# A mixture-of-experts layer on one core: one stationary for the two parts of each expert's 48-row block, with GpSimd's and VectorE's order changed around it

## Chip, core and metric

The kernel runs on one core of a Trainium2 chip. The time is device microseconds of one execution; the table gives the median of three runs. The five engines are TensorE (PE), VectorE (DVE), ScalarE (ACT), GpSimd (POOL) and SyncE (SP). Times inside a profile count from the span's start.

## What is computed

A transformer layer over 1024 rows of 1024 numbers, in float32: a mixer, a cross attention and a grouped mixture of experts, each followed by a layer norm. The change lies in the last part alone:

```python
y = jnp.zeros_like(t)
for e in range(N_EXPERTS):                      # 16 experts, D_EXPERT = 256
    h = jax.nn.silu(t @ w_gate[e]) * (t @ w_up[e])
    y = y + combine[:, e:e + 1] * (h @ w_down[e])
x = layer_norm(DEEPNORM_ALPHA * x + y, ln_moe_g[l], ln_moe_b[l])
```

A router picks a group of four experts for each row and two experts in it, so combine has two entries that are not zero in a row.

## The kernel before

Up to 692 us of the span the kernel works through projection, attention and cross attention and sorts the rows into slots: each of the 16 experts has CAP = 176 slots, whose rows lie in a DRAM buffer (slot_rows, `xs_dram`). The function `experts` then takes the experts one after the other, one step each. The first four and the last two are written out, the ten between run in a loop of two. The 176 rows of an expert stand as a block c = 0 of 128 rows and a block c = 1 of 48 rows (`B1`). A step goes as follows.

TensorE computes gate and up for half m = 0 and m = 1 of the 256 hidden columns into h_ps (L2004), turns the next expert's rows with `turn` (L1985, L1987) into rowsT_ps, and computes the down product into y_ps (L2016 to L2018). Float32 precision of down is had from three products of fp32r parts: h_hi with e_dn_hi, h_hi with e_dn_lo, h_lo with e_dn_hi. So each block c, each half j of the 1024 output columns and each half f of the hidden columns takes three matmuls over 512 columns, 24 in a step. The four sums (c, j) share three banks of y_ps; (1, 1) takes the bank of (0, 0) once VectorE has read it.

ScalarE makes silu (L2055), h_hi (L2058), copies the turned rows to xgT (L2039, L2040), makes e_dn_hi for the next expert (L2044) and, from the fifth expert on, the sum of squares of each row for the layer norm (L2071).

VectorE multiplies silu by up (L2128), makes h_lo (L2130), writes the finished rows of the expert before with `put_out` (L2097, both blocks behind the second h_lo), works out which slots hold a row's second expert (`know_high`, `place`), makes the row sums z = y x weight + earlier sum with their accumulators (L2147, four passes over 512 columns), the means (L2102), `centre` (L2108), and splits the next e_dn into e_dn_lo (L2082, four passes). A row's low expert stores z to a DRAM buffer (slot_sums, `z_dram`), and its high expert, at least four steps later, takes that z as the earlier sum. The first four experts have no high rows and so no layer norm.

GpSimd reads weight and ids of the next expert's slots (`read_fields`, L1922, L1924), gathers the earlier sums with two indirect DMAs over the rows in SBUF (`gather_low`, L1929), makes rstd from the squares (L1950, L1953), and scatters the finished rows to out with two indirect DMAs as `put_out` has made them (L1956). Then it waits until they have landed and only then signals `out_free`, on which the next `put_out` waits.

SyncE issues the next e_down_raw load when e_dn_lo is made, the gate and up load two experts ahead when gate and up are done, the two stores of z as they are made, and behind them the two fetches of the rows of the expert after next (L1898, L1880):

```python
for c in range(2):
    hold(z_made, n(4, 2 * c + 6))
    sp.dma_start(k.z_dram[bass.ds(n(CAP, c * P), ROWS[c]), :], z[c][:]).then_inc(z_stored, 16)
if not is_one_of_last(e, 2):
    hold(placed_at, n(1, 1))
    fetch(n(CAP, 2 * CAP), b)
```

All semaphore values are written out by hand: n, h and g_ turn the step's number into the count to wait for. Each engine works its list in order, so a wait holds up all that stands behind it on that engine.

## Time and profile before

| | us |
|---|---|
| median of 3 runs | 977.92 (973.67 to 980.97) |
| profiled execution | 977.82 |
| its span | 976.0 |
| TensorE busy | 941.4, 96% of the span |
| VectorE busy | 591.0, 61% |
| ScalarE busy | 350.9, 36% |
| GpSimd busy | 196.5, 20% |
| mean granted TensorE clock | 0.99 of 2.4 GHz |

The profile is of one execution. Matmuls are pipelined and their ends are modelled, so it is the distance of their starts that tells their cost. The experts take the span from 692 us to the end. In the rows further down a row of a timeline gives start, duration, engine, line, operation, result and inputs; in brackets stands how long the engine was idle before it and what ended the idle time.

### The profile page before, as it was taken

To read this page: it belongs to the slowest core of one execution; us is meant where nothing else is said; L and a number is where in the kernel's file an instruction comes from. 1 tells how busy PE (TensorE), PEld (TensorE's weight loads), DVE (VectorE), ACT (ScalarE), POOL (GpSimd) and SP (SyncE) were. 2 spreads that over 40 slices of the span, in tenths; PEclk is the share of its full clock that TensorE was granted. 3 is DMA by queue.
4 is the path that set the end of the run, shared out by engine and by line. 5 is a ranking of instruction groups with operands and counts; after the bars stand their busy time and mean duration, and the time that the engine had idled before them with its cause. 6 is when DMAs were issued, how large, how long until landed. Compare 5 with 4: busy or idle time off the path is not lost. (4 is left out here: it accounts for less than half of the span.)

```text
span 976.0 us, 15660 instructions
## 1 busy us (share of the span) xinstructions
PE 941.4 (96%) x5655; PEld 798.5 (82%) x5655; DVE 591.0 (61%) x1263; ACT 350.9 (36%) x737; POOL 196.5 (20%) x256
## 2 busy tenths in 40 slices
PE   7999999999999999999999999998999999999993
PEld 6899888778778888888868888878889898989882
DVE  6744341588677775756656455476343567677674
ACT  6123031345575555300043333320322334444441
POOL 0013100122241120122200000005200243342444
PEclk9999999999999999999999999999899999999998
DMA  9122010001699502600223000046688989898962
GB/s 306 64 87 87 1 62 5 1 1 41 255 412 378 177 23 66 259 1 1 87 90 130 1 1 1 16 158 255 232 293 249 318 280 299 289 323 323 308 247 91
DMA packets 67278, 151.60 MB, mean 155 GB/s; under 512 B 8720, under 2 KB 16144, under 8 KB 67216
## 3 DMA queue, kind: packets, MB, share of 16 engines
q1 hardware_dynamic: 59920, 133.82, 39.0%
q0 software_dynamic: 7296, 16.95, 4.6%
q8 instruction: 39, 0.64, 0.3%
q14 instruction: 23, 0.19, 0.1%
HBM read 107.62 MB, written 52.03 MB: 164 GB/s over the span
## 5 line engine op out<-in xcount | busy, mean ns | idle before, releaser
L2004 PEld LDWEIGHTS h_ps<-xgT,e_gate_up 128*128 128x128 f32 x1024 | 155.6, 192 | 4.7 <-issue 2.4
L2004 PE MATMUL h_ps<-xgT,e_gate_up 128*128 128x176 f32 x1024 | 157.1, 315 | 2.4 <-DVEq L2112 2.4
L270 PE MATMUL unit_ps<-whi,xhi 128*128 128x512 f32 (+1 forms) x256 | 98.2, 384 | 6.1 <-DVE wlo L308 6.1
L271 PE MATMUL unit_ps<-wlo,xhi 128*128 128x512 f32 (+1 forms) x256 | 97.9, 382 | 0.0
L272 PE MATMUL unit_ps<-whi,xlo 128*128 128x512 f32 (+1 forms) x256 | 97.7, 382 | 0.0
L270 PEld LDWEIGHTS unit_ps<-whi,xhi 128*128 128x128 f32 x256 | 48.6, 190 | 13.8 <-DVE xlo L352 6.1
L2147 DVE SCALAR_TENSOR_TENSOR z<-y_ps,slot_weight,x_rows 128x512 f32<-128x512 f32 (+1 forms) x64 | 45.6, 746 | 22.5 <-PE y_ps L2018 21.9
L272 PEld LDWEIGHTS unit_ps<-whi,xlo 128*128 128x128 f32 x256 | 48.6, 190 | 7.8
L271 PEld LDWEIGHTS unit_ps<-wlo,xhi 128*128 128x128 f32 x256 | 48.6, 190 | 7.5
L2016 PE MATMUL y_ps<-e_dn_hi,h_hi 128*128 128x512 f32 (+1 forms) x128 | 52.1, 407 | 0.2
L2018 PE MATMUL y_ps<-e_dn_hi,h_lo 128*128 128x512 f32 (+1 forms) x128 | 50.3, 393 | 0.0
L2017 PE MATMUL y_ps<-e_dn_lo,h_hi 128*128 128x512 f32 (+1 forms) x128 | 50.0, 391 | 0.0
L2128 DVE TENSOR_TENSOR h<-silu_g,h_ps 128x176 f32<-128x176 f32 x32 | 10.7, 333 | 56.7 <-ACT silu_g L2055 56.7
L2055 ACT ACTIVATE silu_g<-h_ps 128x176 f32<-128x176 f32 x32 | 10.2, 318 | 93.0 <-PE h_ps L2004 85.8
L2071 ACT ACTIVATE ln_junk<-z,z_neg_mean 128x1024 f32<-128x1024 f32 (+1 forms) x24 | 27.6, 1152 | 39.8 <-DVE z_neg_mean L2102 33.3
L1046 PE MATMUL t_ps<-constants,prob 128*128 128x128 f32 x288 | 41.2, 279 | 0.6 <-DVE prob_T L1194 0.4
L1063 PEld LDWEIGHTS o_ps<-prob_T,mla_v 128*64 128x64 f32 x576 | 30.8, 136 | 12.9 <-DVE prob_T L1194 8.8
L1063 PE MATMUL o_ps<-prob_T,mla_v 128*64 128x128 f32 x576 | 38.5, 278 | 3.0 <-DVE prob_T L1194 2.4
L2082 DVE TENSOR_TENSOR e_dn_lo<-e_down_raw,e_dn_hi 128x512 fp32r<-128x512 f32 x64 | 39.7, 678 | 0.8 <-ACT e_dn_hi L2044 0.8
L1194 DVE COPY prob_T<-t_ps 128x512 f32<-128x512 f32 (+3 forms) x48 | 29.7, 619 | 14.0 <-PE t_ps L1046 13.9
L1116 ACT ACTIVATE prob_T<-t_ps 128x128 f32<-128x128 f32 (+3 forms) x48 | 21.0, 437 | 46.9 <-PE t_ps L1046 46.9
L2044 ACT ACTIVATE e_dn_hi<-e_down_raw 128x512 fp32r<-128x512 f32 x64 | 35.2, 637 | 5.9 <-DVE ln_tmp L2119 4.4
(346 smaller groups left out, 2136.8 us busy)
## 6 DMA issues: line engine op xcount, KB each, us to landing
e_gate_up<-w_gu SPq DMA_DIRECT2D x16, 2048.0 KB, 10.9
e_down_raw<-w_dn SPq DMA_DIRECT2D x16, 1024.0 KB, 5.7
slot_rows<-zeros SPq DMA_DIRECT2D x22, 522.0 KB, 6.3
slot_sums<-zeros SPq DMA_DIRECT2D x22, 512.0 KB, 6.4
x_rows<-slot_rows SPq DMA_DIRECT2D x16, 522.0 KB, 4.6
slot_sums<-z SPq DMA_DIRECT2D x16, 512.0 KB, 4.1
wraw<-w_in SPq DMA_DIRECT2D x24, 256.0 KB, 4.5
xraw<-xT SPq DMA_DIRECT2D x16, 256.0 KB, 5.1
```

What stands on the lines that cost most here:

```text
L270: pe.matmul(o, hi, whi[:, s, 0:w], start=(s == 0), stop=False)
L271: pe.matmul(o, hi, wlo[:, s, 0:w], start=False, stop=False)
L272: last = pe.matmul(o, lo, whi[:, s, 0:w], start=False, stop=(s == KD - 1))
L1046: last = pe.transpose(tps[:, j, m * P:(m + 1) * P], prob[:, u % 2, j, m * P:(m + 1) * P], ident)
L1063: last = pe.matmul(ops[r, i % 2, (h // 2) * P:(h // 2 + 1) * P], k.v[:, m, h * MV:(h + 1) * MV], src, start=(m == 0), stop=(m == i))
L2004: end = pe.matmul(hps[:, m, gu * CAP:(gu + 1) * CAP], gate_up[:, b, s, w], xT[:, s, :], start=(s == 0), stop=(s == KD - 1))
L2016: pe.matmul(out, hi, dn_hi[:, b, w, :], start=(f == 0), stop=False)
L2017: pe.matmul(out, hi, dn_lo[:, b, w, :], start=False, stop=False)
L2018: return pe.matmul(out, lo, dn_hi[:, b, w, :], start=False, stop=(f == 1))
L2044: act.activation(dn_hi[:, b, s, :], dn_raw[:, s, :], ACT.Copy).then_inc(dn_hi_done, 1)
L2082: dve.tensor_tensor(dn_lo[:, b, s, :], dn_raw[:, s, :], dn_hi[:, b, s, :].bitcast(f32), ALU.subtract).then_inc(dn_lo_done, 1)
L2147: dve.scalar_tensor_tensor(z[c][:, f], yps[r, BANK[u], :], wgt[r, b, c:c + 1], rows[b][r, c, f], ALU.mult, ALU.add, accum_out=zsum[r, c, j ...
```

## The change

The layout of `h_hi` gets room behind the 176 columns: the 48-row block's h_hi stands in columns 128 to 175, zeros in 176 to 191, and its low part in 192 to 239. One matmul with columns 128 to 239 as stationary and e_dn_hi as moving gives the high part's product in partitions 0 to 47 and the low part's in partitions 64 to 111 of the same bank; a second adds h_hi with e_dn_lo to partitions 0 to 47. So 12 matmuls of a step become 8. The two sums of the block get banks of their own, the second of them in rowsT_ps. VectorE adds the two parts in two passes over each half: first low part x weight + earlier sum, then high part x weight + that.

`put_out` is split: block 0 behind the first h multiply, block 1 behind the second half's low parts. GpSimd copies the ids for the scatter to a tile of its own and no longer waits for the scatter to land; `put_out` and that copy wait for the scatter of two experts before. TensorE waits for the row sums of the expert before ahead of its transposes, and for the copy of the turned rows ahead of the last four matmuls. The weights lie in DRAM so that two rows of them stand side by side in one partition (`paired`), 4 KB instead of 2 KB in one piece. `fetch` gets an argument for its blocks, which no call gives.

```diff
+def paired(w):
+    return w.rearrange("p (s t) n -> p s (t n)", t=2)
...
-    hhi = at("h_hi", 146, [P, 2, CAP], f32r)
-    hlo = at("h_lo", 147.5, [P, 2, CAP], f32r)
+    LOW = P + 64
+    hhi = at("h_hi", 150, [P, 2, LOW + B1], f32r)
+    hlo = at("h_lo", 147.5, [P, 2, P], f32r)
...
-    UNITS = [(0, 0), (0, 1), (1, 0), (1, 1)]
-    BANK = [0, 1, 2, 0]
+    BANK = [0, 1]
+        small_sums = [yps[:, 2, :], tps[:, 0, :]]
...
-            def fetch(row, b):
-                for c in range(2):
+            def fetch(row, b, blocks=range(2)):
+                for c in blocks:
...
-                    sp.dma_start(dn_raw[:], A["w_dn"][bass.ds(n(1, 1), 1)].rearrange("a s p n -> p (a s) n")).then_inc(dn_loaded, 16)
+                    sp.dma_start(paired(dn_raw[:]), A["w_dn"][bass.ds(n(1, 1), 1)].rearrange("a s p n -> p (a s) n")).then_inc(dn_loaded, 16)
...
                 pool.tensor_tensor(rs[:], sq[:], half[:], ALU.pow).then_inc(rstd_made, 1)
+                if not lowest(e, 2):
+                    hold(out_scattered[b], h(32, -64))
+                pool.tensor_copy(out_ids[:, b, :], ids[:, b, :, 1]).then_inc(out_ids_made, 1)
+                hold(out_ids_made, g_(1, 1))
                 for c in range(2):
                     hold(out_made, g_(2, c + 3))
-                    pool.indirect_dma_start(A["out"], bass.IndirectOffsetOnAxis(ap=ids[0:ROWS[c], b, c, 1:2], axis=0), o[c][:], None,
-                                            bounds_check=S - 1, oob_is_err=False).then_inc(out_scattered, 16)
-                if not is_one_of_last(e, 2):
-                    hold(out_scattered, g_(32, 32))
-                    pool.sem_inc(out_free, 1)
+                    pool.indirect_dma_start(A["out"], bass.IndirectOffsetOnAxis(ap=out_ids[0:ROWS[c], b, c:c + 1], axis=0), o[c][:], None,
+                                            bounds_check=S - 1, oob_is_err=False).then_inc(out_scattered[b], 16)
...
                 else:
+                    pe.wait_ge(z_made, n(4, 4))
                     turn(1 - b, h(32, 32 * (1 + b)))
...
-                def down(u, f):
-                    c, j = UNITS[u]
+                def down(j, f):
                     w = 2 * f + j
-                    hi, lo = (t[:, f, c * P:c * P + ROWS[c]] for t in (hhi, hlo))
-                    out = yps[0:ROWS[c], BANK[u], :]
+                    hi, lo, out = hhi[:, f, 0:P], hlo[:, f, :], yps[:, BANK[j], :]
...
+                def small_down(j, f):
+                    w, sums = 2 * f + j, small_sums[j]
+                    if f:
+                        pe.matmul(sums[0:B1], hhi[:, f, P:CAP], dn_lo[:, b, w, :], start=False, stop=False)
+                    last = pe.matmul(sums[0:64 + B1], hhi[:, f, P:LOW + B1], dn_hi[:, b, w, :], start=(f == 0), stop=(f == 1))
+                    if f == 0:
+                        last = pe.matmul(sums[0:B1], hhi[:, f, P:CAP], dn_lo[:, b, w, :], start=False, stop=False)
+                    return last
...
-                for u, free in ((0, 4), (1, 2), (2, 3)):
-                    pe.wait_ge(z_made, n(4, free))
-                    down(u, 0)
+                pe.wait_ge(z_made, n(4, 4))
+                down(0, 0)
+                down(1, 0)
+                pe.wait_ge(small_lo_done, n(2, 1))
+                small_down(0, 0)
                 pe.wait_ge(hlo_done, n(2, 2))
-                for u in range(3):
-                    down(u, 1).then_inc(ysum, 1)
-                pe.wait_ge(z_made, n(4, 5))
-                down(3, 0)
-                down(3, 1).then_inc(ysum, 1)
+                down(0, 1).then_inc(ysum, 1)
+                down(1, 1).then_inc(ysum, 1)
+                pe.wait_ge(small_lo_done, n(2, 2))
+                small_down(0, 1).then_inc(ysum, 1)
+                if not last:
+                    pe.wait_ge(x_done, n(1, 2))
+                small_down(1, 0)
+                small_down(1, 1).then_inc(ysum, 1)
...
-            def put_out(n, blocks=range(2)):
+            def put_out(n, h, e, b, blocks):
                 dve.wait_ge(rstd_made, n(1, 1))
-                dve.wait_ge(out_free, n(1, 1))
+                if not lowest(e, 2):
+                    dve.wait_ge(out_scattered[b], h(32, -64))
...
                     dve.tensor_tensor(hh[:, m, :], act_g[:, m, :], hps[:, m, CAP:2 * CAP], ALU.mult).then_inc(hmul, 1)
+                    if not lowest(e) and m == 0:
+                        put_out(g_, h, e, b, [0])
                     dve.wait_ge(hhi_done, n(2, m + 1))
-                    dve.tensor_tensor(hlo[:, m, :], hh[:, m, :], hhi[:, m, :].bitcast(f32), ALU.subtract).then_inc(hlo_done, 1)
-                    if last:
-                        put_out(g_, [m])
-                if not lowest(e) and not last:
-                    put_out(g_)
+                    dve.tensor_tensor(hlo[:, m, :], hh[:, m, 0:P], hhi[:, m, 0:P].bitcast(f32), ALU.subtract).then_inc(hlo_done, 1)
+                    dve.tensor_tensor(hhi[:, m, LOW:LOW + B1], hh[:, m, P:CAP], hhi[:, m, P:CAP].bitcast(f32), ALU.subtract)\
+                       .then_inc(small_lo_done, 1)
+                if not lowest(e):
+                    put_out(g_, h, e, b, [1])
...
+                for j in range(2):
+                    row_sums(j, 0, j, yps[:, BANK[j], :], rows[b][:, 0, 512 * j:512 * j + 512], zsum[:, 0, j:j + 1], z_made)
+                if last:
+                    mean(0, n)
+                for j in range(2):
+                    row_sums(2 + j, 1, j, small_sums[j][64:64 + B1], rows[b][0:B1, 1, 512 * j:512 * j + 512], None, half_made)
+                for j in range(2):
+                    dve.wait_ge(half_made, n(2, j + 1))
+                    row_sums(2 + j, 1, j, small_sums[j][0:B1], z[1][:, 512 * j:512 * j + 512], zsum[0:B1, 1, j:j + 1], z_made)
                 if last:
                     mean(1, n)
+                    centre(0, g_)
                     centre(1, g_)
```

`row_sums` is the pass of L2147 with the sum, the earlier sum and the accumulator given.

## Rows read from the trace of the kernel before

**Rows 1.** The page, part 1: busy time of each engine.

```profile
PE 941.4 (96%) x5655; PEld 798.5 (82%) x5655; DVE 591.0 (61%) x1263; ACT 350.9 (36%) x737; POOL 196.5 (20%) x256
```

**Rows 2.** Windows: stretch, length, each engine's busy us, granted clock, DMA share, GB/s.

```profile
828.12:845.18 17.06, 16.98 (x105) 14.65 (x104) 11.87 (x24) 7.50 (x15) 6.36 (x8) 1.00 0.89 292
...
861.96:878.71 16.75, 16.75 (x106) 14.72 (x105) 11.91 (x24) 7.38 (x15) 6.61 (x8) 1.00 0.91 326
...
945.74:976.00 30.26, 15.54 (x89) 12.99 (x87) 17.56 (x30) 6.31 (x12) 14.46 (x14) 0.84 0.28 96
```

**Rows 3.** Timeline of TensorE, one step (start, duration, line, operation, tiles).

```profile
861.96 9.71 PE L2004 MATMUL h_ps<-xgT,e_gate_up 128*128 128x176 f32 x64
871.51 1.04 PE L1985 MATMUL rowsT_ps<-constants,x_rows 128*128 128x128 f32 x8
...
873.10 0.49 PE L2016 MATMUL y_ps<-e_dn_hi,h_hi 128*128 128x512 f32 x1
873.43 0.39 PE L2017 MATMUL y_ps<-e_dn_lo,h_hi 128*128 128x512 f32 x1
...
878.71 0.46 PE L2004 MATMUL h_ps<-xgT,e_gate_up 128*128 128x176 f32 x2
```

**Rows 4.** Groups by line and form, weight loads of down (busy us, mean ns).

```profile
L2017 PEld LDWEIGHTS y_ps<-e_dn_lo,h_hi 128*128 128x128 f32 x64 | 12.0, 188 | 2.0
```

**Rows 5.** Timeline of VectorE, the same step, and the last scaling pass.

```profile
862.16 0.74 DVE L2147 SCALAR_TENSOR_TENSOR z<-y_ps,slot_weight,x_rows 48x512 f32<-48x512 f32 x1 [0.64 <-PE y_ps L2018]
...
862.84 0.33 DVE L2102 SCALAR_TENSOR_TENSOR z_neg_mean<-z_sums,minus_share 128x1 f32<-128x1 f32 x2
863.11 2.47 DVE L2108 SCALAR_TENSOR_TENSOR ln_tmp<-z,z_neg_mean,ln_g 128x1024 f32<-128x1024 f32 x2
865.51 2.48 DVE L2082 TENSOR_TENSOR e_dn_lo<-e_down_raw,e_dn_hi 128x512 fp32r<-128x512 f32 x4
867.92 0.32 DVE L2128 TENSOR_TENSOR h<-silu_g,h_ps 128x176 f32<-128x176 f32 x1
...
872.06 0.34 DVE L2128 TENSOR_TENSOR h<-silu_g,h_ps 128x176 f32<-128x176 f32 x1 [2.98 <-ACT silu_g L2055]
...
873.13 2.48 DVE L2097 SCALAR_TENSOR_TENSOR ln_out<-ln_tmp,z_rstd,ln_b 128x1024 f32<-128x1024 f32 x2
...
966.61 1.27 DVE L2160 SCALAR_TENSOR_TENSOR ln_tmp<-ln_tmp,z_rstd,ln_b 48x1024 f32<-48x1024 f32 x1 [0.89 <-POOL z_rstd L1970]
```

**Rows 6.** Timeline of GpSimd: the same step, and two operations of other steps.

```profile
866.80 1.24 POOL L1922 COPY slot_weight<-x_rows 128x2 f32 x1 [5.78 <-DMA out<-ln_out,slot_ids]
...
869.44 1.15 POOL L1929 DMA_INDIRECT x_rows<-slot_sums,slot_ids  x1 [1.07 <-issue]
...
872.37 0.72 POOL L1953 TENSOR_TENSOR z_rstd<-z_squares,minus_half 128x2 f32<-128x2 f32 x1 [0.28 <-POOL z_squares L1950]
...
781.93 2.04 POOL L1950 TENSOR_SCALAR z_squares<-z_squares 128x2 f32<-128x2 f32 x1 [3.03 <-ACT ln_junk L2071]
...
948.13 4.64 POOL L1929 DMA_INDIRECT x_rows<-slot_sums,slot_ids  x1 [1.02 <-DMA slot_sums<-z]
```

**Rows 7.** Timeline of ScalarE: copies of the turned rows, end of the squares.

```profile
856.43 1.09 ACT L2039 ACTIVATE xgT<-rowsT_ps 128x512 f32<-128x512 f32 x2 [0.42 <-PE rowsT_ps L1987]
...
865.62 0.19 ACT L2071 ACTIVATION_READ_ACCUMULATOR ln_junk<-z,z_neg_mean 48x1 f32 x1
```

**Rows 8.** Timeline of SyncE's queue, the same step: the fetches of rows.

```profile
863.79 0.96 SPq L1880 DMA_DIRECT2D x_rows<-slot_rows  x2
```

**Rows 9.** DMA view: us to landing, windows 846:849, L1880, 764:766.5; rate in 774:778.

```profile
x_rows<-slot_rows SPq DMA_DIRECT2D x1, 195.8 KB, 5.9
...
DMA to landing us min/median/max: 3.4/5.1/6.1
...
e_down_raw<-w_dn SPq DMA_DIRECT2D x1, 1024.0 KB, 8.1
...
DMA packets 787, 1.61 MB, mean 403 GB/s; under 512 B 6, under 2 KB 6, under 8 KB 787
```

More of the change, by code:

```diff
@@ L1324, in _ @@
             sp.wait_ge(w_lo, XH)
-            sp.dma_start(k.e_dn[:], A["w_dn"][0].rearrange("s p n -> p s n")).then_inc(k.dn_loaded, 16)
+            sp.dma_start(paired(k.e_dn[:]), A["w_dn"][0].rearrange("s p n -> p s n")).then_inc(k.dn_loaded, 16)
             sp.dma_start(k.g3[:], over(A["ln_moe_g"], [P, D])).then_inc(k.gains_loaded, 16)
@@ L1820, in experts @@
     ids = at("slot_ids", 149.53125, [P, 2, 2, 2], i32)
+    out_ids = at("out_ids", 149.75, [P, 2, 2], i32)
     zsum = at("z_sums", 149.5625, [P, 2, 2])
@@ L1849, in alone @@
             step(lambda a, c: e * a + c, lambda a, c: e // 2 * a + c, lambda a, c: (e - NG) * a + c, e, e % 2)
-        for e in range(NG):
+        for e in range(NG + 2):
             alone(e)
-        with eng.Fori(NG // 2, NE // 2 - 1) as i:
+        with eng.Fori(NG // 2 + 1, NE // 2 - 1) as i:
             for b in range(2):
@@ L1857, in steps, with lowest @@
             alone(e)
-    def lowest(e):
-        return isinstance(e, int) and e < NG
+    def lowest(e, more=0):
+        return isinstance(e, int) and e < NG + more
     def is_one_of_last(e, count):
@@ L1973, in finish_last @@
                     pool.indirect_dma_start(A["out"], bass.IndirectOffsetOnAxis(ap=ids[0:ROWS[c], (NE - 1) % 2, c, 1:2], axis=0), tmp[c][:], None,
-                                            bounds_check=S - 1, oob_is_err=False).then_inc(out_scattered, 16)
+                                            bounds_check=S - 1, oob_is_err=False).then_inc(out_scattered[(NE - 1) % 2], 16)
             steps(pool, step)
-            pool.wait_ge(out_scattered, 32 * (NE - NG))
+            for b in range(2):
+                pool.wait_ge(out_scattered[b], 16 * (NE - NG))
             pool.wait_ge(z_stored, 32 * NE + 128)
@@ L2143, in step, with row_sums @@
                 dve.wait_ge(z_stored, n(32, 128))
-                for u, (c, j) in enumerate(UNITS):
-                    r, f = slice(0, ROWS[c]), slice(512 * j, 512 * j + 512)
+                def row_sums(u, c, j, sums, rest, out, made):
+                    r = slice(0, ROWS[c])
                     dve.wait_ge(ysum, n(4, u + 9))
-                    dve.scalar_tensor_tensor(z[c][:, f], yps[r, BANK[u], :], wgt[r, b, c:c + 1], rows[b][r, c, f], ALU.mult, ALU.add,
-                                             accum_out=zsum[r, c, j:j + 1]).then_inc(z_made, 1)
-                    if last and u == 1:
-                        mean(0, n)
-                    if last and u == 2:
-                        centre(0, g_)
+                    dve.scalar_tensor_tensor(z[c][:, 512 * j:512 * j + 512], sums, wgt[r, b, c:c + 1], rest, ALU.mult, ALU.add, accum_out=out)\
+                       .then_inc(made, 1)
+                for j in range(2):
[7 more added lines that the diff above has]
+                    row_sums(2 + j, 1, j, small_sums[j][0:B1], z[1][:, 512 * j:512 * j + 512], zsum[0:B1, 1, j:j + 1], z_made)
                 if last:
                     mean(1, n)
+                    centre(0, g_)
                     centre(1, g_)
```

26 lines of the change are left out of this document (14 added, 12 removed).

## Prediction

> **What bounds the kernel now.** I read the page first: TensorE is busy 96% of the span [rows 1]. That is an average over stages, so next the windows view, one stretch per expert, over the loop that the diff touches. In step 861.96:878.71 TensorE is busy for the whole 16.75 us while VectorE has 11.9 us of work, ScalarE 7.4 and GpSimd 6.6 [rows 2]; the others of the loop are alike. TensorE's timeline says what fills such a step: gate and up matmuls 9.55 us (861.96 to 871.51), transposes of the next rows 1.59 us, and 24 down matmuls from 873.10 to 878.71, 5.61 us [rows 3]. They follow each other by 0.229 us, the first by 0.33 [rows 3]. So in the steady step nothing waits for another engine: a matmul taken away is worth its 0.229 us at once, as long as the others follow. Two places are otherwise. Step 828.12:845.18 took 17.06 us, 0.31 more: the six matmuls of its last sum had to wait for their bank of y_ps. And from 945.74 on comes the last expert with the tail, 30.26 us, where TensorE is busy for half the time only [rows 2].
>
> I count below from t = 0, the start of a step's gate and up matmuls (861.96 in the step shown).
>
> **TensorE.** The 48-row block loses one of three matmuls for each (j, f): 12 become 8, so a step has 20 down matmuls. The new stationary has 112 columns; loading 128 columns takes 188 ns [rows 4], which bounds it from above and lies under the 0.229 us in which a 512-column matmul goes by, so it stays hidden. Gain per step 4 x 0.229 = 0.92 us: the step goes from 16.75 to 15.83. Fifteen steps end in the next gate and up: 15 x 0.92 = 13.8 us. The 0.31 us of bank wait goes too, since each of the four sums now has a bank of its own. The new waits of TensorE: z_made (all rows of the expert before) ahead of the transposes is met at t = 2.3 of 9.55; x_done ahead of the last four matmuls, which start at 14.9, is met some 2 us early (ScalarE's two large copies from rowsT_ps took 1.09 us from 856.43 [rows 7]; with the third they end at about 12.8). Behind the first stand the transposes and all of down, so what is late there is late for everyone.
>
> **VectorE.** Today, in t: last row sum 0.20, means 0.88, centre 1.15, split of e_dn 3.55, first h multiply 5.96, second h multiply 10.10, put_out 11.17 [rows 5]. Added are two more passes over 48x512. The trace does not show them without the accumulator; a pass with it holds the engine 0.68 us (862.16 to 862.84, [rows 5]), and I take that as the upper end and 0.6 (a quarter of the 2.40 us of split's four passes over 512 columns, [rows 5]) as the lower: 1.34 us. Added too are two 48-column subtractions, while h_lo narrows from 176 to 128: a pass of this kind over 176 columns takes 0.34 us (the h multiply, [rows 5]), so each costs between nothing and 0.34 us net, and I take 0.1. That makes 11.9 + 1.5 = 13.4 us in 15.83. Order matters more than the sum. The second half sum must await TensorE's last matmul, so half, z2 and z3 run 0.20 to 2.23; means, centre and split then end at 7.3 and the first h multiply comes at 7.3 instead of 5.96. Then put_out(0), 1.20 us, and the subtractions: 9.1 if rstd is there, before the second multiply is due at 10.10. put_out(1) ends at 12.5, place at 12.9, and the first row sum is due at 15.83 - 1.86 = 13.97. So VectorE has about 1 us to spare ahead of the second multiply and again ahead of the row sums. If the first is used up, TensorE still loses nothing until h_lo of the second half, here made at 11.1, is later than 13.1, when TensorE comes to it; behind h_lo stand put_out(1), place and the row sums.
>
> **GpSimd.** rstd must now be there at t = 7.6, and today it is made at 11.1 [rows 6]: two gathers from 869.44 on stand in front of it, and these wait because read_fields starts only at 866.80, after 5.78 us of waiting for the scatter to land [rows 6]. The change takes that wait away (the one put in its place is on the scatter of two experts before). So the chain moves up: put_out(1) done 12.5, its scatter 1.0 us later (the idle time ahead of an indirect DMA is 1.07) to 14.4, the first gather 1.7 us after that (866.80 to 869.44, less the 1 us by which the copy was held up), gathers at 0.3 to 2.7 of the next step, squares ready from ScalarE at 5.2 (today 865.81, 2.7 us after the end of the row sums [rows 7]), rstd about 6.5. But GpSimd's small operations stall behind VectorE's centre and split: z_squares took 2.04 us until split ended, and a gather begun in centre took 4.64 us instead of 1.15 [rows 6]. So z_squares waits for split's end at 7.3 and rstd comes at 8.4; put_out(0) then ends at 9.65, the subtractions at 9.97, still ahead of 10.10. If also the second gather is caught by centre (it starts at 1.7, or 2.3 when the new out_ids copy, 0.2 us, is itself held up behind put_out; centre starts at 2.5), rstd is at 9.6, h_lo of the second half at 12.2, row sums at 13.97 just met. No loss on TensorE either way, but the slack is used.
>
> The Trainium skill, page "SBUF — State Buffer", section "Who interferes with whom", says that a VectorE instruction with two SBUF inputs and a GpSimd instruction that reads SBUF exclude each other, and that whoever starts first keeps the port for its whole instruction. By that rule the gathers are safe when they start before centre and lost until split's end when they do not; the trace agrees with its 4.64 us gather, and the sum would be the same by rule and by row in the forecast case and would be rival 2 in the other.
>
> **Queues.** In the queue of SyncE the order is the same as before: each expert's z stores already stand ahead of the fetch of rows, and the new argument of fetch is given nowhere. That part of the title changes nothing. What moves is when: today the last z is ready at 0.95 and the fetches issue at 1.83 and about 2.35 [rows 8]; then 2.3, 3.2 and 3.7. The second fetch lands 5.9 us after issue (3.4 to 6.1 for all, [rows 9]): 9.6, against transposes due at 9.55. Today it has 1.3 us to spare. If the landing is set by the backlog in front of it, it moves by less. I take 0.1 us for each of ten loaded steps, 1.0 us; ends 0 and 0.3. w_dn's load issues 0.3 us after split's end, 7.6 instead of 6.3, and lands in 8.1 at worst [rows 9], 15.7; ScalarE's split of four passes then ends at about 18.0, which is 2.2 of the next step, and VectorE needs it at 4.9. Hidden; the gate and up load is issued two experts ahead. Weights now come in rows of 4 KB instead of 2 KB; at 2 KB the DMA engines already move 403 GB/s in a full stretch [rows 9], where whole steps need some 320, so I count nothing. A gain could only shorten the backlog ahead of the rows, which is in the lower end, 0.
>
> **Tail.** With t from the last gate and up: put_out(0) no longer comes late for the second multiply (the 4.64 us gather is out of the way), down ends 0.9 us sooner, but VectorE has two more passes (1.34) in the chain of row sums, means, centre and output, and centre(0) now follows mean(1). I get the second scaling pass at 20.6 against 20.87 today (966.61 [rows 5]): with the scatters behind it the end moves by -0.5 to +0.5. Count 0.
>
> **Sum.** The profiled execution took 977.8 us (span 976.0 and 1.8 around it), the runs' median is the same to 0.1. 977.8 - 13.8 - 0.3 + 1.0 = 964.7 us. Its own range, with rows late 0 to 0.3 us a step and the tail +-0.5: 963 to 967.5.
>
> **Rivals.**
> 1. Rows late. The loop row sums, fetch, landing, transposes, 11 down matmuls, row sums is 9.9 us and the landing L. With L = 5.9 it is 15.8, equal to TensorE's step. If L is 6.2, the step is 16.1: 14 x 0.3 = 4 us lost, 968 to 970. For it: the fetch meets the gathers, which move up to the same stretch. Against: the scatters, which were there, move away.
> 2. The VectorE and GpSimd loop bounds. If both gathers fall behind centre and split: centre and split 4.8, gathers 2.4, rstd 1.3, put_out(0) 1.2, subtractions, multiply, h_hi and h_lo 1.4, put_out(1) 1.2, place 0.4, row sums and means 4.3: 17.0. Only the first four steps then gain: 975 to 977. For it: the gather of 4.64 us. Against: at such a step GpSimd would get to its first gather before centre again, so it does not hold itself.
> 3. Slower. One mechanism: the second fetch of rows lands as late as the latest w_dn load, 8.1 us after issue [rows 9], since it now sits nearer to the gate and up load's end and the gathers. Then the step is 18.0 and 14 of them add 17.5 us: about 994. It turns slower than before at L = 6.85 and by 1% at 7.5; none of the row fetches shown exceeds 6.1.
> That the change does nothing at all can't be for TensorE: the four matmuls are gone.
>
> **Chances.** Forecast 0.66, rival 1 0.15, rival 2 0.12, rival 3 0.07. Leaving out rivals 2 and 3 leaves out 0.19; forecast and rival 1 span 963 to 970, and the runs before lie 3 to 4 us from their median (973.67 and 980.97), of which a median of runs keeps some: 960 to 972. About 1% is what a measurement of this kernel can tell from no change: faster by more (under 968.1) is the forecast and a third of rival 1, 0.71; within it 0.22; slower 0.07.
>
> **What would show it.** Gate and up starts 15.8 us apart; 20 down matmuls at 0.229 us; no gap of TensorE ahead of the transposes (a gap there and its size is rival 1, or 3); GpSimd's gathers under 1.2 us each, started before centre (4 us ones mean rival 2); z_squares stretched to split's end; no wait of TensorE for h_lo. Wrong would be: a pace of the 112-column matmuls above 0.24, or put_out pushing the second h multiply past 12.

## The result and the profile after

The changed kernel took 964.48 us (median of 3 runs, 962.45 to 965.53), the kernel before 977.92. The ratio is 0.9869, 95% interval 0.9839 to 0.9899. The prediction was 964.7 us, in a range of 960 to 972. The total is right, but it is made up differently than I had worked it out: less was gained in the steady steps, something in the tail. One thing the change does is missing from its description above: the first six experts are written out instead of four (`for e in range(NG + 2)`), and the loop runs over eight. Every variant of the changed kernel below has this too.

The profiled execution took 962.45 us, span 960.7. Part 1 of its page; its VectorE has 22.7 us more work than before and its TensorE 15.5 us less [rows 1]:

```profile
PE 925.9 (96%) x5591; PEld 791.8 (82%) x5591; DVE 613.7 (64%) x1328; ACT 350.7 (37%) x737; POOL 206.1 (21%) x267
```

The windows view of the kernel after: an ordinary step, a step with late rows, and the last expert with the tail (stretch, length, busy time of PE, PEld, DVE, ACT and POOL, granted clock, DMA share, GB/s). They answer to [rows 2].

```profile
833.93:849.89 15.96, 15.96 (x101) 14.41 (x100) 13.30 (x29) 7.47 (x15) 7.21 (x10) 1.00 0.88 306
...
882.04:899.13 17.09, 16.07 (x101) 14.41 (x100) 13.38 (x29) 7.36 (x15) 8.39 (x10) 1.00 0.95 361
...
931.97:960.70 28.73, 14.55 (x85) 12.79 (x83) 20.84 (x38) 6.30 (x12) 12.47 (x13) 0.84 0.29 102
```

The first is as forecast (15.83 us, VectorE 13.4). The second is 1.1 us longer, and in it TensorE is idle for 1.02 us. TensorE's timeline in it, the step that starts at 882.04:

```profile
890.69 1.06 PE L2012 MATMUL h_ps<-xgT,e_gate_up 128*128 128x176 f32 x6
892.77 1.09 PE L1993 MATMUL rowsT_ps<-constants,x_rows 128*128 128x128 f32 x8 [1.02 <-DMA x_rows<-slot_rows]
```

Gate and up are done, and the transposes wait for the rows of the next expert. All starts of gate and up, read from TensorE's timelines, in us after the one before (the first step is another matter, below):

| step | before | after |
|---|---|---|
| 1 | 18.53 | 18.56 |
| 2 to 7 | 16.75 each | 15.92, then 15.87 to 15.88 |
| 8 to 12 | 16.74, 17.06, 16.78, 16.75, 16.74 | 16.51, 16.38, 15.96, 16.21, 15.94 |
| 13, 14, 15 | 16.75, 16.79, 16.75 | 17.09, 15.88, 16.96 |
| 2 to 15 | 234.85 | 226.22 |
| tail | 30.26 | 28.73 |

The fourteen steps 2 to 15 gained 8.6 us of the 12.2 that I had for them (14 x 0.92 + 0.3 - 1.0). The tail gained 1.5 us of which I had none. And 5.2 us of the difference between the two spans lie ahead of the experts, where the change touches only the loads of the first weights and one memset: the first gate and up starts at 692.36 before and 687.19 after.

### The profile page after: what moved, and what is told of

Read it like the earlier page. It is cut to its first block and busy times, and to the rows that moved or that the text cites. A ratio compares the mean times of both kernels' runs of the same rounds, so it can differ in the third digit from the quotient of the medians.

```text
span 960.7 us, 15514 instructions
## 1 busy us (share of the span) xinstructions
PE 925.9 (96%) x5591; PEld 791.8 (82%) x5591; DVE 613.7 (64%) x1328; ACT 350.7 (37%) x737; POOL 206.1 (21%) x267
## 5 line engine op out<-in xcount | busy, mean ns | idle before, releaser
L2173 DVE SCALAR_TENSOR_TENSOR z<-y_ps,slot_weight,x_rows 128x512 f32<-128x512 f32 (+1 forms) x48 | 34.9, 750 | 27.1 <-PE y_ps L2025 26.5
L1046 PEld LDWEIGHTS t_ps<-constants,prob 128*128 128x128 f32 x288 | 31.4, 141 | 6.9 <-issue 5.4
L2120 DVE SCALAR_TENSOR_TENSOR ln_out<-ln_tmp,z_rstd,ln_b 128x1024 f32<-128x1024 f32 (+1 forms) x24 | 30.6, 1277 | 9.7 <-POOL z_rstd L1959 9.7
L862 ACT ACTIVATE mixT_hi<-s_ps 128x1024 fp32r<-128x1024 f32 x8 | 8.2, 1028 | 69.6 <-DVE s_ps L882 68.3
L1185 DVE TENSOR_REDUCE neg_max<-s_ps 128x1 f32<-128x640 f32 (+3 forms) x32 | 32.8, 1024 | 1.2
```

The source lines that it names most:

```text
L1046: last = pe.transpose(tps[:, j, m * P:(m + 1) * P], prob[:, u % 2, j, m * P:(m + 1) * P], ident)
L1185: dve.tensor_reduce(nmx[:, u % 2, 0:1], s[:, 0:(i + 1) * P], AX.X, ALU.max, negate=True).then_inc(max_ready, 1)
L2120: dve.scalar_tensor_tensor(o[c][:], tmp[c][:], rs[r, c:c + 1], b_[r, :], ALU.mult, ALU.add).then_inc(out_made, 1)
L2173: dve.scalar_tensor_tensor(z[c][:, 512 * j:512 * j + 512], sums, wgt[r, b, c:c + 1], rest, ALU.mult, ALU.add, accum_out=out)\
```

## Experiments

### Both kernels again, and which part of the difference is theirs

> The kernel before, unchanged, to see what varies by itself. Theory 1 (the 5.2 us by which the first expert started sooner in the changed kernel's profile, 692.4 to 687.2, are variation between executions): here too the start of the first gate and up moves by some us from one profile to the next, somewhere in 685 to 695, and the ratio is 1.000 +- 0.003. Theory 2 (they come from the 4 KB rows of the weights' loads): the start is within 1 us of 692.4.

> The changed kernel, unchanged. Theory 1: the first gate and up may start anywhere in 685 to 695; the fifteen steps take 244.8 +- 1.5 us as in the first profile, with TensorE waiting in some of them for the rows' load ahead of the transposes. Theory 2: start within 1 us of 687.2. Ratio 0.984 to 0.990.

> The changed kernel once more, beside the other three: ratio to before 0.987 to 0.990, steps two to fifteen 226.3 +- 0.5 us with waits for rows of 0.3 to 1.1 us in four or five of them.

No edit in these. The kernel before took 977.39 us (ratio 1.0007, 0.9984 to 1.0031); the kernel after 966.55 (0.9889, 0.9848 to 0.9931) and, in a later comparison, 963.69 (0.9869, 0.9850 to 0.9889). What their profiles say, in us:

| | before | before again | after | after again | after, third |
|---|---|---|---|---|---|
| first gate and up starts | 692.36 | 687.66 | 687.19 | 688.53 | 689.79 |
| steps 2 to 15 | 234.85 | 236.17 | 226.22 | 226.44 | 225.0 |
| tail | 30.26 | 29.74 | 28.73 | 28.66 | 28.7 |

So the 5.2 us ahead of the experts are no effect of the change: the kernel before starts its experts at 687.66 as well, and over all profiles of this study the start lies between 687.2 and 692.8, whatever the kernel. The first step varies too, from 17.6 to 22.4 us, and is longest where the first rows came late. In the second profile of after it took 21.87 us, so that the fifteen steps together took 248.3 us and not the 244.8 +- 1.5 that I expected. The third profile's 225.0 us lie outside the 226.3 +- 0.5 expected, with only two waits for rows (0.40 and 1.15 us). What repeats is 9.6 us in steps 2 to 15 (235.5 less 225.9, the means) and 1.3 us in the tail. The first step has four matmuls less as well; its 0.9 us are counted and not measured, since the step varies by more. With them this makes 11.8 us, a ratio of 0.988, and that is where the three comparisons lie (0.9869, 0.9889, 0.9869).

### The four matmuls back

> The changed kernel with four more 512-column matmuls a step, on the 16 zero columns of the stationary (they add zero), so TensorE has its 24 down matmuls back and all else is as changed. If the four matmuls are the whole gain and late rows only eat into it: steps of 16.75 to 16.8 us with no wait for rows (they have 0.92 us more), so 15 x 0.92 = 13.8 less the 4.5 us of waits for rows that go away: 9 us slower than the changed kernel, ratio to before 0.995 to 0.997. If the gain came from the order of GpSimd and VectorE: it stays near 0.987.

```diff
                     if f:
+                        pe.matmul(sums[0:LOW - CAP], hhi[:, f, CAP:LOW], dn_hi[:, b, w, :], start=False, stop=False)
                         pe.matmul(sums[0:B1], hhi[:, f, P:CAP], dn_lo[:, b, w, :], start=False, stop=False)
                     last = pe.matmul(sums[0:64 + B1], hhi[:, f, P:LOW + B1], dn_hi[:, b, w, :], start=(f == 0), stop=(f == 1))
                     if f == 0:
+                        pe.matmul(sums[0:LOW - CAP], hhi[:, f, CAP:LOW], dn_hi[:, b, w, :], start=False, stop=False)
```

The kernel after with four matmuls more in a step, whose stationary is the sixteen columns of zeros: the count is that of before, everything else is that of after. 976.84 us, ratio 0.9997 (0.9974 to 1.0019). Its TensorE timeline at the end of a step:

```profile
877.06 0.40 PE L2033 MATMUL rowsT_ps<-e_dn_hi,h_hi 128*112 128x512 f32 x1
877.30 0.40 PE L2035 MATMUL rowsT_ps<-e_dn_hi,h_hi 128*16 128x512 f32 x1
877.54 0.39 PE L2036 MATMUL rowsT_ps<-e_dn_lo,h_hi 128*48 128x512 f32 x1
877.77 0.40 PE L2031 MATMUL rowsT_ps<-e_dn_lo,h_hi 128*48 128x512 f32 x1
...
878.46 1.80 PE L2012 MATMUL h_ps<-xgT,e_gate_up 128*128 128x176 f32 x11
```

Stationaries of 16, 48 and 112 columns follow each other by 0.23 to 0.24 us, as those of 128 do: at 512 moving columns the width of the stationary makes no difference here. Of the fourteen steps behind the first, twelve take 16.82 to 16.89 us, the last two 17.27 and 17.16. I had expected 16.75 to 16.8 us and a ratio of 0.995 to 0.997; with the matmuls back the kernel is no faster than before. So in the steps the four matmuls are the whole gain, and the order, the queues and the row length together bring none of it. The tail is another matter: here it takes 29.1 us, still 0.9 us less than the 30.0 of before (the mean), so most of what the tail gained doesn't come from the matmuls; the steps, 236.4 us together against 235.5, give that back. The run shows one thing more: at 16.82 us a step TensorE's waits for rows behind the first step are down to two of 0.2 us. The rows come late because the step has become shorter.

### The order back

> The changed kernel with GpSimd's and VectorE's order as before: put_out of both blocks behind the second h_lo, and GpSimd waits until the scatter has landed before it goes on. If the order is what makes room for the two added passes: the loop put_out 2.4, scatters 3.3, landing 5, read_fields 1.6, gathers 3.5, rstd 1.2 is about 17 us against 15.87, row sums come late, and the ten steps with a layer norm take 16.3 to 17 us: 5 to 10 us slower than the changed kernel. If TensorE's matmuls alone decide: the same as the changed kernel within 1 us.

```diff
-                    if not lowest(e) and m == 0:
-                        put_out(g_, h, e, b, [0])
...
-                    put_out(g_, h, e, b, [1])
+                    put_out(g_, h, e, b, [0, 1])
...
+                if not is_one_of_last(e, 2):
+                    hold(out_scattered[b], h(32, -32))
```

`put_out` for both blocks behind the second h_lo, and GpSimd waits again until the scatter has landed. 979.77 us, ratio 1.0030 (1.0014 to 1.0047), 16 us more than the kernel after beside it (963.69). My expectation, 5 to 10 us, was too small. Steps 2 to 4 still take 15.87 us; among the later ones are 17.25, 17.70, 18.20, 17.80, 23.18 and 21.64. GpSimd and VectorE in two such steps; columns as in [rows 5] and [rows 6]:

```profile
845.44 2.75 POOL L1928 COPY slot_weight<-x_rows 128x2 f32 x1 [5.99 <-DMA out<-ln_out,out_ids]
...
861.87 1.22 POOL L1928 COPY slot_weight<-x_rows 128x2 f32 x1 [3.81 <-DVE z L2173]
863.18 3.56 POOL L1930 TENSOR_SCALAR slot_ids<-slot_where 128x4 int32<-128x4 f32 x1
867.82 1.14 POOL L1935 DMA_INDIRECT x_rows<-slot_sums,slot_ids  x1 [1.08 <-issue]
...
870.74 0.72 POOL L1959 TENSOR_TENSOR z_rstd<-z_squares,minus_half 128x2 f32<-128x2 f32 x1 [0.28 <-POOL z_squares L1956]
```

```profile
861.75 2.47 DVE L2133 SCALAR_TENSOR_TENSOR ln_tmp<-z,z_neg_mean,ln_g 128x1024 f32<-128x1024 f32 x2
864.15 2.48 DVE L2106 TENSOR_TENSOR e_dn_lo<-e_down_raw,e_dn_hi 128x512 fp32r<-128x512 f32 x4
...
871.59 2.47 DVE L2122 SCALAR_TENSOR_TENSOR ln_out<-ln_tmp,z_rstd,ln_b 128x1024 f32<-128x1024 f32 x2 [2.73 <-POOL z_rstd L1959]
...
877.16 0.75 DVE L2173 SCALAR_TENSOR_TENSOR z<-y_ps,slot_weight,x_rows 128x512 f32<-128x512 f32 x1 [2.76 <-DMA x_rows<-slot_sums,slot_ids]
```

This is the state of rival 2, brought about here by the old order: GpSimd begins its fields only when the scatter has landed (5.99 us of waiting at 845.44; a step later it has the rows' sums to wait for as well) and so, at 861.87, 0.12 us after VectorE has begun centre; the ids (0.24 us otherwise) last until split ends; the gathers come at 867.8, rstd at 870.7 to 871.5, `put_out` behind it, and the row sums wait for the gathered rows until 877.16. The z stores and the fetch of rows go late with them, and TensorE then waits 4.18 us for rows at 888.16. So without the new order the four matmuls are lost again. The kernel before held 16.75 us a step with the old one, and here steps 5 to 15 take 17.8 us in the mean, so the shorter step alone doesn't explain it. That it is the two added VectorE passes for which the order makes room is argued from this; no run took the passes away. The Trainium skill, page "SBUF — State Buffer", section "Who interferes with whom", says that a VectorE instruction with two SBUF inputs contends with a GpSimd instruction that reads SBUF; the 3.56 us of an operation over 128x4 elements beside centre and split agree with it.

### Longer pieces of the weights

> The kernel before with only the 4 KB rows of weights. Theory 1: steps stay at 16.75 us, ratio 0.997 to 1.001. Theory 2: the first gate and up starts about 5 us sooner, ratio about 0.995. Either way the gate and up load lands in 9.4 us instead of 10.9, as in the changed kernel.

> The changed kernel with weights in rows of 2 KB again. The kernel before with 4 KB rows measured 0.4% slower than without. If 4 KB rows harm: this is 2 to 4 us faster than the changed kernel and has fewer waits for rows. If they help by shortening the gate and up load from 10.9 to 9.4 us ahead of the rows: 1 to 4 us slower, with longer waits for rows. If neither: within 1 us.

```diff
-sp.dma_start(gate_up[:, b], A["w_gu"][bass.ds(n(1, 2), 1)].rearrange("a s p n -> p (a s) n")).then_inc(gu_loaded[b], 16)
+sp.dma_start(paired(gate_up[:, b]), A["w_gu"][bass.ds(n(1, 2), 1)].rearrange("a s p n -> p (a s) n")).then_inc(gu_loaded[b], 16)
```

The first is the kernel before with pieces of 4 KB (here its core; w_dn and the order in DRAM go with it), the second the kernel after with pieces of 2 KB. Alone, the pieces bring nothing: 979.45 us, ratio 1.0042 (1.0018 to 1.0066), slightly slower and outside the 0.997 to 1.001 expected; steps 2 to 15 take 236.6 us against 234.85 and 236.17 without them, so the steps don't tell where the 0.4% go. Without them the kernel after takes 966.36 us, ratio 0.9909 (0.9886 to 0.9932), against 963.69 (0.9850 to 0.9889) beside it; steps 2 to 15 take 227.96 us against 225.0, with a wait for rows of 2.01 us. The load of gate and up does land sooner with them. From the DMA view, pieces of 4 KB (after; before it was 10.9, and 9.8 in the kernel before with the longer pieces):

```profile
e_gate_up<-w_gu SPq DMA_DIRECT2D x16, 2048.0 KB, 9.4
```

Each of the four runs with pieces of 2 KB (965.28 to 968.81) is slower than each of the four of the kernel after beside it (961.77 to 964.18), which speaks for a help of the pieces in the changed kernel. But the intervals of the ratios still touch, and another comparison had the kernel after at 966.55; so the 2.7 us are not settled.

### Why the rows are late: the issue time

> The changed kernel with the rows' fetch taken apart: block 0 as soon as its two row sums are made, block 1 as soon as the two half sums have read it, and only then the store of z's block 1. So the fetches issue at about t = 0.6 and 1.5 of a step instead of 3.2 and 3.7. If the waits ahead of the transposes come from the late issue (rival 1 of the prediction): no such wait from the second step on, fourteen steps of 15.87 = 222.2 us instead of 226.3, ratio to before 4 us lower than the changed kernel's, 0.983 to 0.985. If they come from the load of the DMA engines (gathers, gate and up): waits of 0.3 to 1.1 us stay, ratio as the changed kernel's.

```diff
-                for c in range(2):
+                store(0)
...
-                    fetch(n(CAP, 2 * CAP), b)
+                    fetch(n(CAP, 2 * CAP), b, [0])
+                    hold(half_made, n(2, 2))
+                    fetch(n(CAP, 2 * CAP), b, [1])
+                store(1)
```

The use of the new argument of `fetch`: block 0 of the rows right behind the store of z block 0, block 1 when VectorE has read the low halves, the store of z block 1 last. The fetches issue at t = 0.4 and about 1.3 in place of 3.4 and 3.9. 962.98 us, ratio 0.9868 (0.9851 to 0.9884), the same as the kernel after and not the 0.983 to 0.985 of an issue that decides alone. The small waits of steps 8 to 12 are gone (15.87 to 15.90 each; steps 2 to 15 take 224.2 us, against 225.0 to 226.4), but steps 13 and 15 stay at 17.11 and 16.51. TensorE's timeline, and the DMA view of that step (name, queue, operation, count, KB, median us from issue to landing):

```profile
893.55 1.09 PE L1999 MATMUL rowsT_ps<-constants,x_rows 128*128 128x128 f32 x8 [1.04 <-DMA x_rows<-slot_rows]
```

```profile
x_rows<-slot_rows SPq DMA_DIRECT2D x1, 195.8 KB, 9.4
```

Issued almost 3 us sooner, the second fetch lands 9.4 us after its issue instead of 6.8, at the same time: for the two long steps it stands in a line, and the issue time isn't the cause.

### Why the rows are late: the line itself

> The kernel after, with the gate and up load of a step cut to its first half (1 MB in place of 2 MB; the other half of the buffer keeps what an earlier expert left, so the output is not the reference's). In the kernel after, TensorE waits 0.3 to 1.0 us for rows in the steps from 892 and 925 us on, and issuing the fetch 3 us earlier moved only the smaller of these waits. Theory A: the rows are late because the gate and up load, issued at t = 10 and landed near t = 4 of the next step, stands in front of them on the same DMA engines. Then all fifteen steps are 15.87 us apart, no wait for rows is left, and the time falls by what the late rows cost, 3 to 4 us, to about 960. Theory B: they are late for another reason (the many short pieces of the gathers and scatters, or the write of slot_sums): then the long steps at 892 and 925 us stay at 17.1 and 16.5, and the time stays within 1 us of the kernel after.

> The kernel after, with w_gu stored by halves of the hidden columns, so that the first 1 MB of the next gate and up load can be issued when the gate and up of half 0 are done (t = 4.8) and the second at t = 9.6, in place of 2 MB at t = 10. The DMA engines have a lull of some 1.4 us from t = 8.5 on, which this fills. Theory A (the backlog of this load makes the rows late): it lands some 2 to 3 us sooner, the rows behind it too, the waits for rows go, steps of 15.87 us, 3 to 4 us off the kernel after, about 960. w_dn lands up to 2.5 us later, still before its split is due. Theory B (another reason): the long steps stay, no change beyond 1 us.

> Both: the gate and up load in halves and the fetch of block 0 of the rows behind the store of z block 0, of block 1 behind the half sums. Theory A: as with the halves alone, about 960, since no wait is left to take away; at most 0.5 us less. Theory B: as the early fetch alone, 963.

```diff
-sp.dma_start(paired(gate_up[:, b]), A["w_gu"][bass.ds(n(1, 2), 1)].rearrange("a s p n -> p (a s) n")).then_inc(gu_loaded[b], 16)
+sp.dma_start(paired(gate_up[:, b, 0:4]), A["w_gu"][bass.ds(n(1, 2), 1), 0:2].rearrange("a s p n -> p (a s) n")).then_inc(gu_loaded[b], 16)
```

That is the half load; it leaves out half of each expert's gate and up weights. All fourteen steps behind the first take 15.87 to 15.91 us, no wait for rows is left, and step 13 reads, in the windows view:

```profile
883.91:899.79 15.88, 15.88 (x102) 14.46 (x100) 13.31 (x29) 7.48 (x15) 7.43 (x9) 1.00 0.82 277
```

The DMA engines are busy for 0.82 of it in place of 0.95, and the rows come in time with the fetch where it was. This bears out theory A: with 1 MB less on the DMA engines no wait is left. It doesn't show that only this load is in the way, since less of any other traffic was not tried. The median, 962.22 us (ratio 0.9868), is above the 960 expected and shows little of it; in the profiled execution the first step took 21.59 us (rows of the very first fetches late by 2.45 us) and nearly 6 us more than a steady step; from the second step on the profile is 222.3 us where the kernel after has 225.0 to 226.4.

The next edit leaves nothing out. w_gu is stored by halves of the hidden columns, and each half of its load goes out as soon as the gate and up that read it are done:

```diff
+                def load(m):
+                    hold(gsum, n(2, m + 1))
+                    sp.dma_start(gate_up[:, b, 2 * m:2 * m + 2, :], A["w_gu"][bass.ds(n(1, 2), 1), 2 * m:2 * m + 2].rearrange("a q p n -> p (a q) n"))\
+                      .then_inc(gu_loaded[b], 16)
+                if not is_one_of_last(e, 2):
+                    load(0)
                 if not last:
                     hold(dn_lo_done, n(4, 4))
```

So 1 MB of it issues at t = 5.2 in place of 10. From t = 8 to 9.9 the DMA engines of the kernel after move 87 GB/s, against 410 in the 0.6 us behind; windows view, the step that starts at 833.93:

```profile
841.93:843.83 1.90, 1.90 (x15) 1.76 (x14) 1.26 (x2) 0.41 (x2) 0.75 (x2) 1.00 0.55 87
```

Alone this took 963.77 us (0.9895, 0.9858 to 0.9932), a miss of the 960 expected: the waits shrink (0.51, 0.77 and 0.36 us) but stay, and steps 2 to 15 take 224.9 us. With the early fetch as well it took 960.27 us (0.9858, 0.9823 to 0.9894), and no step is longer than 15.88 us.

> The kernel with both edits once more, with more rounds, since its first comparison left an interval that overlaps that of the kernel after. If the backlog of the gate and up load is the cause and both edits together remove it, the profile again shows fourteen steps of 15.87 us behind the first and no wait for rows, steps 2 to 15 sum to 222.2 us against 225 to 226.4 in the three executions of the kernel after, and the time is 3 to 4 us under the 963 to 966 of that kernel, 959 to 961, ratio to before 0.983 to 0.986. If the first execution was a lucky one, late rows are back in the steps from 880 and 912 us on and the time is 962 to 964.

The same kernel once more: 963.11 us against 978.99 of the kernel before beside it, ratio 0.9842 (0.9819 to 0.9865). The ratio is at the expected place; the microseconds are 2 over it, but the runs of before beside it are slower too, and the profiled execution started its experts at 692.76. The steps are those of the first execution: 15.87 to 15.88 each, 222.2 us together. Step 13 in the windows view, and SyncE's queue in the step before it:

```profile
885.00:900.87 15.87, 15.87 (x101) 14.46 (x100) 13.30 (x29) 7.17 (x16) 7.44 (x9) 1.00 1.00 357
```

```profile
868.93 0.37 SPq L1912 DMA_DIRECT2D slot_sums<-z  x1
869.56 1.15 SPq L1887 DMA_DIRECT2D x_rows<-slot_rows  x2
872.21 0.02 SPq L1912 DMA_DIRECT2D slot_sums<-z  x1
874.31 0.40 SPq L1898 DMA_DIRECT2D e_gate_up<-w_gu  x1
876.91 0.40 SPq L1905 DMA_DIRECT2D e_down_raw<-w_dn  x1
879.08 0.37 SPq L1898 DMA_DIRECT2D e_gate_up<-w_gu  x1
```

Here the DMA engines are never idle (share 1.00), TensorE neither. It is the best kernel of the study by its steps, 2.8 to 4.2 us shorter than the three of after; by the medians of whole executions its ratio overlaps with theirs.

### Why steps 13 and 15

In the kernel after, steps 13 and 15 are late in all three profiles. The DMA view of single steps bears on it: packets, MB and the share of the 16 engines; q0 is the queue of GpSimd's gathers and scatters. The kernel after, step 11 and step 13:

```profile
DMA packets 1627, 5.42 MB, mean 334 GB/s; under 512 B 308, under 2 KB 308, under 8 KB 1627
...
q0 software_dynamic: 405, 0.79, 12.7%
```

```profile
DMA packets 1812, 6.17 MB, mean 361 GB/s; under 512 B 309, under 2 KB 309, under 8 KB 1812
...
q0 software_dynamic: 497, 1.16, 17.8%
```

Gathers and scatters move only the slots that hold a row of the kind asked for, and that depends on the data: nothing in steps 2 to 4, 0.3 to 0.8 MB in steps 5 to 12 (0.8 to 0.9 in step 11 of the other two profiles), 1.16 MB in step 13, 0.43 in step 14, 1.34 in step 15. In the kernel with both edits, whose steps are all of one length, step 13 has 1.04 MB and step 15 1.28. The two steps that move most are the two that an early fetch didn't mend. The counts don't explain every late step: step 8 moves 0.5 MB and takes 16.51, 16.65 and 16.25 us in the three profiles of after, and in the second of them the longest step is step 11 (17.17 us, 0.9 MB). That their own gathers and scatters are what tips steps 13 and 15 is read from these counts; no run took them away.

The kernel before has the same line. Its first trace shows 0.97 MB in step 13 and 1.37 in step 15, and no wait of TensorE there. The second time its steps 13 and 15 took 17.69 and 17.01 us, by another path. VectorE's timeline of that kernel:

```profile
910.17 0.75 DVE L2147 SCALAR_TENSOR_TENSOR z<-y_ps,slot_weight,x_rows 128x512 f32<-128x512 f32 x1 [1.49 <-DMA x_rows<-slot_sums,slot_ids]
```

and TensorE's:

```profile
910.99 0.43 PE L2016 MATMUL y_ps<-e_dn_hi,h_hi 128*48 128x512 f32 x1 [0.74 <-DVE z L2147]
```

The gathered sums came late, the row sums with them, and the last sum of TensorE waited for its bank. This wait the change takes away for good, since each sum has a bank of its own; in its place stands the wait for the rows.

## Why the prediction was right, and where its sum was not

**TensorE.** The removal is right: 20 down matmuls follow each other by 0.23 to 0.24 us. The timeline of TensorE at the end of a step of the kernel after:

```profile
848.73 0.40 PE L2032 MATMUL y_ps<-e_dn_hi,h_hi 128*112 128x512 f32 x1
848.96 0.40 PE L2032 MATMUL rowsT_ps<-e_dn_hi,h_hi 128*112 128x512 f32 x1
849.20 0.40 PE L2034 MATMUL rowsT_ps<-e_dn_lo,h_hi 128*48 128x512 f32 x1
849.43 0.40 PE L2031 MATMUL rowsT_ps<-e_dn_lo,h_hi 128*48 128x512 f32 x1
849.66 0.40 PE L2032 MATMUL rowsT_ps<-e_dn_hi,h_hi 128*112 128x512 f32 x1
849.89 0.61 PE L2012 MATMUL h_ps<-xgT,e_gate_up 128*128 128x176 f32 x3
```

From the first down matmul (845.16) to the next gate and up 4.73 us pass, against 5.61 before [rows 3]: 0.88 us a step, not 0.92, and fifteen times 13.2 us, not 13.8. The bank wait of 0.31 us is gone.

**VectorE and GpSimd.** The chain came out as written. In the step that starts at 833.93 I had rstd at t = 8.4, `put_out(0)` done at 9.65, the second multiply at 10.10, `put_out(1)` done at 12.5. VectorE's timeline:

```profile
842.57 1.28 DVE L2120 SCALAR_TENSOR_TENSOR ln_out<-ln_tmp,z_rstd,ln_b 128x1024 f32<-128x1024 f32 x1 [0.84 <-POOL z_rstd L1959]
843.77 0.28 DVE L2156 TENSOR_TENSOR h_lo<-h,h_hi 128x128 fp32r<-128x128 f32 x1
843.97 0.20 DVE L2157 TENSOR_TENSOR h_hi<-h,h_hi 128x48 fp32r<-128x48 f32 x1
844.09 0.33 DVE L2152 TENSOR_TENSOR h<-silu_g,h_ps 128x176 f32<-128x176 f32 x1
...
845.17 1.27 DVE L2120 SCALAR_TENSOR_TENSOR ln_out<-ln_tmp,z_rstd,ln_b 48x1024 f32<-48x1024 f32 x1
...
849.49 0.75 DVE L2173 SCALAR_TENSOR_TENSOR z<-y_ps,slot_weight,x_rows 48x512 f32<-48x512 f32 x1
850.16 0.75 DVE L2173 SCALAR_TENSOR_TENSOR z<-rowsT_ps,slot_weight,x_rows 48x512 f32<-48x512 f32 x1
```

`put_out(0)` holds VectorE to 843.77 (t = 9.84), the second multiply comes at 10.16, `put_out(1)` ends at 12.4. A half pass without the accumulator holds the engine 0.67 us, the upper of my two ends. GpSimd's timeline:

```profile
839.49 2.04 POOL L1956 TENSOR_SCALAR z_squares<-z_squares 128x2 f32<-128x2 f32 x1 [3.41 <-ACT ln_junk L2093]
841.81 0.72 POOL L1959 TENSOR_TENSOR z_rstd<-z_squares,minus_half 128x2 f32<-128x2 f32 x1 [0.28 <-POOL z_squares L1956]
...
849.87 1.14 POOL L1935 DMA_INDIRECT x_rows<-slot_sums,slot_ids  x1 [1.08 <-issue]
851.31 0.94 POOL L1935 DMA_INDIRECT x_rows<-slot_sums,slot_ids  x1 [0.30 <-issue]
```

z_squares is stretched to split's end (841.5) as forecast, rstd is used at 842.57 (t = 8.64), and both gathers are through at t = 2.4, 0.3 us before centre begins at 852.56. In step 8 of all three profiles the margin is smaller: the second gather starts at t = 2.0, centre at 2.67, and the gather ends at 2.96, in its usual 0.94 us: begun ahead of centre, it isn't held. The order-back experiment shows what it costs where the margin is gone.

**Rows: the term that was too small.** I had 0.1 us for each of ten steps, 1.0 us. Steps 2 to 15 of the three executions of after stand 4.0, 4.2 and 2.8 us above fourteen times 15.87 (222.2 us). The mechanism, the second fetch of rows against transposes due at t = 9.55, is the one I named; so is the lateness of its issue (3.4 and about 3.9, forecast 3.2 and 3.7). What failed is the landing: I took 5.9 us from one step, 6.1 at most, where step 13 has 6.8, and spread the excess evenly. It comes in lumps, TensorE waiting for up to 1.15 us at a time, most often in the steps whose gathers and scatters move most. My remark that the backlog might move with the issue is what the early fetch shows, in the other direction: in step 13, sooner issued is not sooner landed. Rival 1 asked for 0.3 us in every step, 4 us in all: in its sum it is what happened, in its place it isn't, since most steps lose nothing; and its total of 968 to 970 us didn't come, as the tail and the waits of the kernel before gave something back.

**Tail.** I counted nothing and it gained 1.3 us in the means, by a path that I had wrong. The second scaling pass comes at t = 22.50 (954.47), not 20.6, and 1.6 us later than before [rows 5]:

```profile
949.92 2.47 DVE L2131 SCALAR_TENSOR_TENSOR ln_tmp<-z,z_neg_mean,ln_g 128x1024 f32<-128x1024 f32 x2
952.32 1.27 DVE L2193 SCALAR_TENSOR_TENSOR ln_tmp<-ln_tmp,z_rstd,ln_b 128x1024 f32<-128x1024 f32 x1
954.47 1.28 DVE L2193 SCALAR_TENSOR_TENSOR ln_tmp<-ln_tmp,z_rstd,ln_b 48x1024 f32<-48x1024 f32 x1 [0.88 <-POOL z_rstd L1977]
```

Before, one centre pass ran while TensorE was still at the last sum; now both stand behind all row sums, and z_squares of block 1, 1.04 us before, takes 2.12 beside them. Yet from the end of GpSimd's last instruction (957.91; 970.05 before) to the end of the span only 2.8 us pass, where before it was 5.9. The trace shows what lies in that time. The DMA view of the kernel before from 972 us on has two packets, both of the kind that it calls instruction, and no data; they start at 972.8 and 972.9, about 3.2 us before the end:

```profile
q8 instruction: 1, 0.02, 2.1%
q14 instruction: 1, 0.01, 0.8%
```

All three profiles of the kernel before and its variant with longer pieces have this load there, and 5.6 to 6.0 us from that last instruction to the end; all eleven profiles of the changed kernel and its variants, that with the four matmuls back included, have none there, and 2.7 to 2.8 us. So the tail is 1.6 us longer to its last scatter and about 3.1 us shorter behind it: a load of code no longer falls at the very end. That the two experts written out more are what moved it is likely and was not tried.

**The total.** 964.7 was forecast from 13.8 + 0.3 - 1.0 = 13.1 us of gain. The repeated profiles give 13.2 for the matmuls, 1.0 for waits that the kernel before had (234.85 and 236.17, in the mean 235.5, against fourteen times 16.75, 234.5), less 3.7 for the rows, and 1.3 for the tail: 11.8. Two terms of mine were off and two were missing: the rows took 3.7 us in place of 1.0 and the matmuls gave 13.2 in place of 13.8, while the tail and most of the waits of the kernel before stood at nothing. They nearly cancel. The error of 1.3 us that is left is within what a median moves (the three medians of after lie 2.9 us apart). The exact agreement of 964.48 with 964.7 is luck.

## What to carry to other kernels

A part of a stationary that is small can be put beside another part of the same moving operand: at 512 moving columns a matmul costs 0.23 us with 16, 48, 112 or 128 columns, so count matmuls, not stationary columns. Before a step is made shorter, look at the slack of every transfer in the step that moves the most, not in a typical one, and at the traffic that depends on the data. And where a transfer is late, try first whether an earlier issue makes it land earlier; if it does not, something is in line before it, and the lull of the DMA engines is the place to send that something. Here it took both: the halves without the earlier fetch still left waits.

## What the runs showed of the hardware

- A wait for rows of 1.0 us did not shrink when the fetch was issued almost 3 us sooner (landing 9.4 us in place of 6.8); it went when other traffic was taken off (DMA share 0.82 for 0.95), and when the big load was cut in two and sent into the lull and the fetch issued early as well (share 1.00 with no wait at all).
- Beside VectorE's passes with two SBUF inputs, GpSimd's computation of ids over 128x4 elements took 3.56 us in place of 0.24, and z_squares over 128x2 elements 2.04 us in place of 0.19, each ending within about 0.1 us of VectorE's last such pass, so held over several VectorE instructions in a row. It isn't always the last: in the step that starts at 804.69 of the order-back kernel the ids took 1.08 us and ended when centre's first pass did.
- Pieces of 4 KB in place of 2 KB let 2 MB land in 9.4 us in place of 10.9 in the changed kernel and in 9.8 us in the kernel before, which yet was 0.4% slower with them.
- At the end of the kernel before, two packets of instructions (24 KB) were loaded about 3 us before the end of the span, with nothing else moving; where no load fell there, the span ended 2.7 us behind GpSimd's last instruction in place of 5.6 to 6.0.
- All but identical code up to the experts ended between 687.2 and 692.8 us of the span in the profiles of this study; a comparison of two single profiles has to take this out first.
